# Attention of the first block: each pair of heads in three steps, of one group of two query tiles and two single ones, in place of four steps

## What is computed

```python
for l in range(DEPTH):                       # DEPTH = 2
    proj = rms_norm(x, attn_norm[l]) @ w_in[l]
    ...
    o_fox  = fox_attention(fq, fk, fv, cum_logf)          # 6 heads of 64, a forget gate added to the logits
    o_diff = diff_attention(dq, dk, dv, lam)              # 4 heads, two softmaxes of 32 dims each, p1 - lam * p2
    o_dsa  = dsa_attention(sq, sk, sv, iq, ik, iw, topk)  # 6 heads of 64, only the 128 best keys of a query
    x = x + concatenate([o_fox, o_diff, o_dsa]) @ w_out[l]
    gate, up = split(rms_norm(x, ffn_norm[l]) @ w_gate_up[l], 2)
    x = x + (silu(gate) * up) @ w_down[l]

# each attention, for a tile of 128 queries, causal:
p = softmax(where(mask, q @ k.T * scale (+ gates), -inf)); out = p @ v
```

## Time and profile before

| | |
|---|---|
| median of three runs | 2233.86 us |
| the profiled execution | 2233.64 us |
| its span | 2231.7 us |
| PE busy | 2178.9 us, 98% of the span |
| PEld, DVE, ACT, POOL busy | 1786.5, 1263.0, 901.3, 291.8 us |
| first layer's attention, from its first turn to its last values | 155.6 to 282.6 us |
| second layer's attention | 823.8 to 950.8 us |

### The profile page before, as it was taken

How to read it: one execution, slowest core, us unless ns; L and a number is a source line. 1 busy time by engine, 2 the same in 40 slices (tenths; PEclk the granted TensorE clock), 3 DMA queues, 4 the chain that set the end, 5 groups by cost and what they waited for, 6 DMA issues and landing times.

```text
span 2231.7 us, 31549 instructions
## 1 busy us (share of the span) xinstructions
PE 2178.9 (98%) x12794; PEld 1786.5 (80%) x12794; DVE 1263.0 (57%) x1751; ACT 901.3 (40%) x1574; POOL 291.8 (13%) x215
## 2 busy tenths in 40 slices
PE   7999999999999999999999999999999999999998
PEld 6886688778888776688778888989888887888777
DVE  5687648983224687648984226422666636212794
ACT  3447843222213447843222223232565524212673
POOL 3001213121222001322121000000010000000230
PEclk9999999999999999999999999999999999999999
DMA  5220016543563220016543321132000122321221
GB/s 164 90 71 2 1 57 207 173 148 86 143 176 93 90 71 1 2 59 205 182 145 81 138 96 58 49 98 75 16 23 9 53 76 92 123 70 57 72 72 57
DMA packets 149107, 194.28 MB, mean 87 GB/s; under 512 B 43165, under 2 KB 96426, under 8 KB 148962
## 3 DMA queue, kind: packets, MB, share of 16 engines
q1 hardware_dynamic: 110288, 169.83, 23.3%
q10 hardware_dynamic: 38514, 22.26, 3.7%
q0 software_dynamic: 160, 0.16, 0.0%
HBM read 180.51 MB, written 11.72 MB: 86 GB/s over the span
## 4 chain that ended last, share of the span: by engine, by line
PE 90%; DVE 4%; ACT 3%; issue 2%; DMA 0%; ACTq 0%; POOLq 0%; DVEq 0%
PE ps L535 69%; PE ps L2757 3%; PE ps L1890 3%; PE ps L2774 2%; PE ps L2786 2%; PE ps L2304 1%; PE ps L2261 1%; PE ps L2290 1%; DVE probs_t L2105 1%; PE ps L2762 1%; PE ps L1924 1%; ACT probs_t L2863 1%; DVE neg_max L2072 1%; PE ps L542 1%; PE ps L2760 1%
## 5 line engine op out<-in xcount | busy, mean ns | idle before, releaser
L500 DVE TENSOR_TENSOR w_low<-w_raw,w_high 128x2048 fp32r<-128x2048 f32 (+4 forms) x140 | 303.4, 2167 | 487.5 <-ACT w_high L495 487.3
L495 ACT ACTIVATE w_high<-w_raw 128x2048 fp32r<-128x2048 f32 (+4 forms) x140 | 253.2, 1809 | 577.2 <-PE ps L535 560.6
L535 PE MATMUL ps<-h_hi,w_high 128*128 128x512 f32 (+1 forms) x1168 | 439.7, 376 | 3.1 <-DVE w_low L500 2.1
L535 PE MATMUL ps<-h_lo,w_high 128*128 128x512 f32 (+1 forms) x1168 | 437.2, 374 | 0.0
L535 PE MATMUL ps<-h_hi,w_low 128*128 128x512 f32 (+1 forms) x1168 | 436.7, 374 | 0.0
L535 PEld LDWEIGHTS ps<-h_hi,w_high 128*128 128x128 f32 x1168 | 219.9, 188 | 53.9 <-issue 10.7
L535 PEld LDWEIGHTS ps<-h_hi,w_low 128*128 128x128 f32 x1168 | 219.8, 188 | 39.6
L535 PEld LDWEIGHTS ps<-h_lo,w_high 128*128 128x128 f32 x1168 | 220.0, 188 | 39.1 <-issue 0.5
L535 PE MATMUL ps<-w_high,h_hi 128*128 128x512 f32 (+3 forms) x576 | 214.2, 372 | 0.6 <-DVE h_lo L3159 0.6
L535 PE MATMUL ps<-w_low,h_hi 128*128 128x512 f32 (+3 forms) x576 | 211.6, 367 | 0.0
L535 PE MATMUL ps<-w_high,h_lo 128*128 128x512 f32 (+3 forms) x576 | 211.4, 367 | 0.0
(11 more groups left out here) (389 smaller groups left out, 3681.6 us busy)
## 6 DMA issues: line engine op xcount, KB each, us to landing
w_raw<-in_w_gate_up SPq DMA_DIRECT2D x44, 1024.0 KB, 5.2
ada_w<-in_ada_w SPq DMA_DIRECT2D x24, 1024.0 KB, 5.2
w_raw<-in_w_down SPq DMA_DIRECT2D x20, 1024.0 KB, 4.8
w_raw<-in_w_in SPq DMA_DIRECT2D x16, 1024.0 KB, 5.1
w_raw<-in_c_in_w SPq DMA_DIRECT2D x16, 1024.0 KB, 5.7
w_raw<-in_w_out SPq DMA_DIRECT2D x8, 1024.0 KB, 4.8
w_raw<-in_ab_in_w SPq DMA_DIRECT2D x8, 1024.0 KB, 5.1
masked_scratch<-mask_table ACTq DMA_DIRECT2D x8, 512.0 KB, 3.5
```

Source lines behind the costliest of these rows:

```text
L495: e.activation(w_high[j % 2][:, 0:size], w_raw[j % 2][:, 0:size], ACT.Copy).then_inc(sig.w_high_done, 1)
L500: e.tensor_tensor(w_low[j % 2][:, 0:size], w_raw[j % 2][:, 0:size], w_high[j % 2][:, 0:size].bitcast(F32), ALU.subtract).then_inc(sig.w_lo ...
L535: mm = e.matmul(dst, lhs, rhs, start=start and a == 0, stop=stop and a == 2)
```

## The change

A unit now has three steps instead of four. Step 3u holds the query tiles 1 and 0 side by side in one bank for each head (256 + 128 = 384 columns), step 3u + 1 holds tile 2 (384) and step 3u + 2 tile 3 (512). Maxima and exponentials stay one for each tile; transposes, their copy and the values of a step go together. There are three buffers for the transposed probabilities instead of two. For tile 0 the mask and the gates are written ahead of the scores and the scores are added; the copy of the causal mask that the kept keys of tile 0 use moves to keep_mask[:, 1, 256:384]. exps signals each head by itself. The loops run over units, each in two halves: on TensorE scores and masks of step 3u, transposes of the previous unit's steps 1 and 2, a first event of bank 7, values of the previous unit's step 0, a second event, scores and masks of steps 3u + 1 and 3u + 2, transposes of step 3u, the previous unit's wide, and its values of steps 1 and 2. VectorE's 37 rounds are spread over 15 halves, two or three behind the maxima of a half. The square root moves in ScalarE's order to the last unit's first half, and both pair_wide, both pair_finish and the last invert stand behind that unit.

```diff
-        probs1 = [at(f"probs1_{i}", [P, 2, S], F32, PJ_END + 4096 * i) for i in range(3)]
-        probs_t1 = [at(f"probs_t1_{i}", [P, 2, S], F32, PJ_END + 12288 + 4096 * i) for i in range(2)]
+        probs1 = [at(f"probs1_{i}", [P, 2, n], F32, PJ_END + 3072 * i) for i, n in enumerate((384, 384, 512))]
+        probs_t1 = [at(f"probs_t1_{i}", [P, 2, n], F32, PJ_END + 10240 + 3072 * i) for i, n in enumerate((384, 384, 512))]
...
-AHEAD, SETS = 2, 3
-ROUND_STEPS = 30
-EARLY_PARTS = {32: 0, 33: 1, 36: 2}
+TILES = ((1, 0), (2,), (3,))
+PER = len(TILES)
+ROUND_HALVES = 15
+EARLY_PARTS = {16: 0, 17: 1, 18: 2}
...
+        self.group(p, [("q", col(FQ + P * p)), ("k", col(FK + P * p))])
+        self.group(3 + 2 * c, [("q", col(DQ + P * c)), ("k", col(DK + P * c))])
+        self.group(7 + p, ([("d", lambda t: keys_twice[:, t, :])] if p == 0 else []) + [("q", col(SQ_ + P * p))])
+    self.steps = [(u, tiles) for u in range(len(self.units)) for tiles in self.TILES]
...
+    self.first_half = {u: [] for u in range(-1, U + 1)}
+    for i, (u, *_) in enumerate(self.turns):
+        self.first_half[u].append(("turn", i))
+    self.first_half[U - 1] += [("sum", 0), ("sum", 1)]
+    self.first_half[U] += [("pair_wide", 0), ("pair_wide", 1)]
+    for u in range(-1, U + 1):
+        for event in self.first_half[u] + ([("wide", u - 1)] if u > 0 else []):
...
+        self.turns.append((first - 1, dst, src, g))
...
+def parts(self, s):
+    at_ = 0
+    for t in self.steps[s][1]:
+        yield t, at_, (t + 1) * P
+        at_ += (t + 1) * P
...
 def bank(self, s, m):
+    return 2 * (s % self.PER) + m
...
 def tensor(self, e, B, L, ch):
+    def added(s, m, t, a, w, start, stop):
+        u, tiles = self.steps[s]
+        out_ = ps[:, self.bank(s, m), a:a + w]
+        if self.units[u].kind == "dsa":
+            at_ = a if t == 0 else 0
+            return e.matmul(out_, ident_r[:], keep_mask[:, tiles[0], at_:at_ + w], start=start, stop=stop)
+        return e.matmul(out_[:, w - P:w], ident_r[:], causal_r, start=start, stop=stop)
+    def gated(s, m, t, a, w, stop):
+        h = 2 * self.units[self.steps[s][0]].n + m
+        return e.matmul(ps[:, self.bank(s, m), a:a + w], gate_sel[:, h * P:(h + 1) * P], gate_t[:, 0:w], start=False, stop=stop)
 def scores(s):
+        u, tiles = self.steps[s]
+        x, parts = self.units[u], list(self.parts(s))
+        if s >= self.PER:
+            e.wait_ge(sig.turned_second, B["turned_second"] + s - self.PER + 1)
...
+        first = len(parts) == 2
+        if first:
+            for m in range(2):
+                added(s, m, *parts[1], True, False)
+                if x.kind == "fox":
+                    gated(s, m, *parts[1], False)
+        for t, a, w in reversed(parts):
+            last = first and t == 0
+            for m in range(2):
+                e.matmul(ps[:, self.bank(s, m), a:a + w], q[x.rows(m), t * P:t * P + P], k[x.rows(m), 0:w], start=not last, stop=bool(last))
+    def masks(s):
+        u, tiles = self.steps[s]
+        x, part = self.units[u], next(self.parts(s))
+        if x.kind == "dsa" and x.n == 0:
+            e.wait_ge(sig.keep_ready, B["keep_ready"] + tiles[0])
     for m in range(2):
+            mm = added(s, m, *part, False, x.kind != "fox")
     if x.kind == "fox":
         for m in range(2):
+                mm = gated(s, m, *part, True)
 def turn_probs(s):
     for m in range(2):
+            e.wait_ge(sig.probs_ready, B["probs_ready"] + 2 * s + m + 1)
+            for b in range(self.size(s) // P):
+                mm = e.transpose(ps[:, self.bank(s, m), b * P:(b + 1) * P],
+                                 probs1[s % 3][:, m, b * P:(b + 1) * P], ident)
 def values(s):
...
+        for t, a, w in self.parts(s):
+            for kt in range(t + 1):
+                for m in range(2):
+                    mm = e.matmul(ps[64 * m:64 * m + 64, 6, t * P:(t + 1) * P], x.value(m, kt),
+                                  probs_t1[s % 3][:, m, a + kt * P:a + (kt + 1) * P], start=kt == 0, stop=kt == t)
...
+    for u in range(-1, self.U + 1):
+        inside, events = 0 <= u < self.U, self.first_half[u]
+        if inside:
+            scores(3 * u)
+            masks(3 * u)
+        if u == 0:
+            keep_warm(e, 6, 6)
+        if u > 0:
+            turn_probs(3 * u - 2)
+            turn_probs(3 * u - 1)
+        for kind, i in events[0:1]:
+            event(kind, i)
+        if u < 0:
             keep_warm(e, 6, 5)
+        if u > 0:
+            values(3 * u - 3)
+        for kind, i in events[1:]:
+            event(kind, i)
+        if u < 0:
+            keep_warm(e, 6, 5)
+        if inside:
+            scores(3 * u + 1)
+            scores(3 * u + 2)
+            masks(3 * u + 1)
+            masks(3 * u + 2)
+        if u == 0:
+            keep_warm(e, 6, 4)
+        if inside:
+            turn_probs(3 * u)
+        if u > 0:
+            wide(u - 1)
+            values(3 * u - 2)
+            values(3 * u - 1)
...
 def scalar(self, e, B, L, ch):
 def exps(s):
...
+        if s >= self.PER:
+            e.wait_ge(sig.probs_turned, B["probs_turned"] + s - self.PER + 1)
     for m in range(2):
+            for t, a, w in self.parts(s):
+                c = 2 * NT * u + 2 * t + m
+                ins = e.activation(probs1[s % 3][:, m, a:a + w], ps[:, self.bank(s, m), a:a + w], ACT.Exp,
+                                   bias=neg_max[:, c:c + 1], accum_out=sums[:, c:c + 1])
+                if t != tiles[-1]:
+                    ch.step(ins)
+            ins.then_inc(sig.probs_ready, 1)
 def copy_probs(s):
...
+        if s >= self.PER:
+            e.wait_ge(sig.o_ready, B["o_ready"] + s - self.PER + 1)
+        e.activation(probs_t1[s % 3][:], self.both(s, 0, self.size(s)), ACT.Copy).then_inc(sig.turned_second, 1)
...
+    for u in range(-1, self.U + 1):
+        inside, turned = 0 <= u < self.U, [i for kind, i in self.first_half[u] if kind == "turn"]
+        if u > 1:
+            copy_o(u - 2)
+        if u > 0:
+            copy_probs(3 * u - 2)
+            copy_probs(3 * u - 1)
+        for i in turned[0:1]:
+            copy_turned(i)
+        if inside:
+            exps(3 * u)
+        for i in turned[1:]:
+            copy_turned(i)
+        if u == self.U - 1:
+            root()
+        if 2 * u in self.EARLY_PARTS:
+            high_part(self.EARLY_PARTS[2 * u])
+        if inside:
+            exps(3 * u + 1)
+            copy_probs(3 * u)
+        if u > 0:
+            copy_wide(u - 1)
+        if inside:
+            exps(3 * u + 2)
+        if u > 1 and self.units[u - 2].kind == "diff":
+            shift(u - 2)
+        if 2 * u + 1 in self.EARLY_PARTS:
+            high_part(self.EARLY_PARTS[2 * u + 1])
+    copy_o(self.U - 1)
...
 def vector(self, e, B, L, ch):
 def maxima(s):
...
+        for t, a, w in self.parts(s):
+            c = 2 * NT * u + 2 * t
+            ins = e.tensor_reduce(out=neg_max[:, c:c + 2], in_=self.both(s, a, w), op=ALU.max, axis=AX.X, negate=True)
+            if t != tiles[-1]:
+                ch.step(ins)
+        ins.then_inc(sig.max_ready, 1)
...
+    for h in range(2 * self.U + 1):
+        u = h // 2
+        if h == 2 * self.U:
+            for c in range(2):
+                pair_finish(c)
+            invert(u - 1)
+            break
+        if h % 2 == 0:
+            maxima(3 * u)
+            if u:
+                invert(u - 1)
+        else:
+            maxima(3 * u + 1)
+            maxima(3 * u + 2)
+        share = min(rounds, early + (rounds - early) * (h + 1) // self.ROUND_HALVES)
     while done < share:
         top_round(e, ch, 1 + done // ROUNDS)
...
```

More of the change, by code:

```diff
@@ L1107, in vector @@
                         e.wait_ge(sig.parts_ready, B["parts_ready"] + 4)
-                        ch.step(e.tensor_copy(keep_mask[:, 0, 0:P], cst("causal")[:, 384:512]))
+                        ch.step(e.tensor_copy(keep_mask[:, 1, 2 * P:3 * P], cst("causal")[:, 384:512]))
                     if i == self.groups - 1:
@@ L2758, in scores @@
-                    for m in range(2):
-                        if x.kind == "dsa":
-                            mm = e.matmul(ps[:, self.bank(s, m), 0:n], ident_r[:], keep_mask[:, t, 0:n], start=False, stop=True)
-                        else:
-                            mm = e.matmul(ps[:, self.bank(s, m), t * P:n], ident_r[:], causal_r, start=False, stop=x.kind != "fox")
+                    first = len(parts) == 2
[4 more added lines that the diff above has]
+                                gated(s, m, *parts[1], False)
@@ L2811, in pair_wide, with event @@
                     mm.then_inc(sig.pair_wide, 1)
-                for s in range(-4, self.N + 1):
-                    if 0 <= s + self.AHEAD < self.N:
-                        scores(s + self.AHEAD)
-                    if -2 <= s < 1:
-                        keep_warm(e, 6, 2 * s + 6 if s < 0 else 4)
-                    if 0 <= s < self.N:
-                        turn_probs(s)
```

(35 more changed lines are left out.)

94 lines of the change are left out of this document (15 added, 79 removed).

## The result

The changed kernel takes 2238.45 us (median of 20 runs, 2233.25 to 2240.74), the kernel before 2233.82 (20 runs beside it): a ratio of 1.0017, 95% interval 1.001 to 1.0023. That is slower, and at the edge of the 0.2% named ahead: the ratio lies inside it, while the medians are 4.63 us apart, and 2238.45 is just above the 2238.3 of the prediction's band. It is also above the forecast's own range of 2228 to 2237. An execution that ran far longer at a much lower mean clock, one of 2887 us among those of e1, is left out of the ratios. The profiled execution took 2238.79 us, 5.15 more than that of before; its span is 2237.0.

A forecast was written before the change was run, and what follows sets the result against it. TensorE, busy 98% of the span, was taken as the bound, with VectorE and ScalarE close behind. Unit terms summed to -0.8 us a layer, -1.6 for both, from 2233.64 to 2232 us; own range 2228 to 2237 (0.46), outer range 2221 to 2242.

The forecast's parts named there:

- the prediction's band: Whole kernel: times from 2229.4 to 2238.3 us, within 0.2% or 4.5 us, count as no change.
- at full clock: Attention stages: rows read at full clock while the widest tile's rounds run; no term for a lower clock.
- The periods: Unit lengths in one layer: units 0 to 2 -0.6 us, 3 to 6 -1.1, 7 and 8 -1.6, the end +2.5.
- under 12.0: Fox units 1 and 2: 12.4 us each; forecast wrong if their periods are under 12.0 or over 13.0.
- the mark on copies: Forecast wrong if TensorE waits for the copy of step 3u in units without rounds of tile 3.
- the second turn: Units 0, 1, 2, 4 and 6: second turned operand waits 0.6 us for ScalarE's copy, bounds 0 to 1.0.
- TensorE's prices: Cost per group on TensorE: fewer groups and moved wide save 0.6 us a unit; diff unit 9.5 us without turns.
- the forecast's +2.5: Unit 9 and the end: table loads ahead of last exponentials, then an uncovered chain; 20.1 us, +2.5 a layer.
- A: Rival, attention stages: handovers fit, TensorE's content alone decides; 2218 us, half of it 2225; chance 0.32 together with C.
- B: Rival, units 1 to 6: rounds ahead of step 3u + 1's maxima decide; +4.8 us a layer, 2242; chance 0.22.
- C: Rival, the end: table loads don't hold step 29's exponentials, 2 x 2.5 us goes; 2227; chance 0.32 with A.
- "same" and "faster": Whole kernel's chances: same (2229.4 to 2238.3 us) 0.46, faster 0.32, slower 0.22.

The follow-up runs named there:

- e1: Changed kernel with products that change no result filling six of TensorE's waits in each attention stage; 2230.84 us, 0.9985 of the kernel before.
- e2: Changed kernel with the last 28 values ahead of the last wide, as in the old order; 2231.34 us, 0.9983 of the kernel before.
- e5: Changed kernel with e2's end and VectorE's rounds moved forward, no block of three rounds of the widest tile; 2217.80 us, 0.9925 of the kernel before.
- e9: e5 with the second turn moved behind the masks of step 3u + 2 in units 0, 1, 2, 4, 6; 2213.77 us, 0.9905 of the kernel before.
- e7: Kernel before the change, with VectorE's rounds five at a time behind every fourth step instead of one or two behind each; 2323.43 us, single execution.
- e8: Kernel before the change, with its VectorE rounds moved forward in the same measure as in e5; 2237.70 us, 1.0014 of the kernel before.
- e6: e5 with six filling products behind unit 0's first transposes, in its long wait; 2217.76 us, 0.9926 of the kernel before.

## Why the prediction was wrong, step by step

**The clock, which was the step that failed.** The sum has TensorE "at full clock" and takes each wait at its own length. The waits themselves it foresaw: for the copy of step 3u in units 3, 5 and 6, for the keep in unit 7, for the spread at the end. That the products behind such a wait would run at 1.2 GHz stood in no term and in no rival, and it is what turned a gain into a loss: of the 5.2 us by which the profiled span grew, -4.7 are the periods, +8.4 the clock, and 1.6 lie outside the stages. With the clock held up (e1) the kernel takes 2230.84 us, inside the forecast's range. The runs of after bear it out, too: of the 20 executions of after, one with a mean granted clock of 0.996 took 2233.25 us, those with 0.992 and 0.993 took 2238.6 to 2240.7.

The Trainium skill, "TensorE: Matmul & The Clock Gate", section "A second HAM failure mode: psum-queue depth-cycling", says of one kernel that its TensorE, idle briefly but often between groups of products, swung between the two clock levels. The traces here don't bear out that it is the number of waits: two a unit of 0.3 to 0.4 us kept 1.00 before, and after, with fewer but longer ones, the means are 0.94 and 0.96.

**The periods.** At full clock (e1, second layer, from the scores of tile 1 of one unit to those of the next) against the prediction: unit 0 10.55 for 11.0; fox units 1 and 2 11.82 and 11.61 for 12.4 each; unit 3 9.92 for 10.1; unit 4 11.19 for 11.1; 5 and 6 11.57 and 11.72 for 11.5 and 11.6; unit 7 12.72 for 12.7; unit 8 9.92 for 10.4; the end 20.05 for 20.1, counted as the forecast did from unit 9's first scores (19.72 from those of tile 1). The mechanism of most held: VectorE had no idle time in unit 5, the block of three stood between TensorE and its copy, the keep came late in unit 7. The fox units were mis-sized by up to 0.8: by the mark set ahead ("under 12.0") that term is wrong. Met too is the mark on copies: ahead of unit 1's scores TensorE waits 1.06 us for the copy of step 0, and unit 0 has no rounds of tile 3, though the prediction's own chain for unit 0 had that wait in it. Of the 0.8, 0.2 is the second turn, whose wait was not 0.6:

```profile
847.00 0.66 PE L2754 MATMUL ps<-con,proj 128*128 128x128 f32 x4 [0.36 <-ACT q_turned L2892]
```

The rest is content, most of it the scores (next paragraph). All errors over 0.1 lie on one side, and at full clock the stages came out 2.1 and 2.6 us shorter than before where 0.8 was forecast. One term was missing the other way: with masks and gates ahead of tile 0's scores, a stage's first scores come 3.25 us behind its first product, against 2.78 before. (The terms for unit 3 add up to 10.2, not 10.1.)

**TensorE's prices.** 14 transposes to the next group 1.65 (887.96 to 889.61; 1.64 forecast), 12 values 0.80, 6 transposes and the wide 1.21 (892.61 to 893.82), both as forecast. The group costs that the prediction read from the earlier trace rows for transposes and values carry over to larger groups. What it overlooked is that scores have one too. Its own prices of 0.41, 0.62, 0.84 and 1.06 us rise by 0.22 a tile, which leaves 0.19 for the group, and scores also fall from four groups to two. The scores of tiles 2 and 3 together take 1.70 (890.41 to 892.11), where 1.90 was forecast, those of tiles 0 and 1 0.85 (886.83 to 887.68) for 1.03, and four masks in a row 0.50 (892.11 to 892.61) for 0.56. So a diff unit has 9.0 us of TensorE's work instead of 9.5: this term was mis-sized by nearly 0.5 us in every unit. (The eight changes of tiling mode that the prediction counts for the new unit are those of a unit with a second turn between values and scores; without it there are seven.)

**VectorE.** The timeline of unit 5, second layer: 

```profile
888.66 1.01 DVE L2979 TENSOR_REDUCE neg_max<-ps 128x2 f32<-128x512 f32 x2
...
890.00 0.68 DVE L2642 MAX8 top<-score 128x8 f32<-128x512 f32 x1
...
891.73 0.70 DVE L2642 MAX8 top<-score 128x8 f32<-128x512 f32 x1
...
893.47 0.69 DVE L2642 MAX8 top<-score 128x8 f32<-128x512 f32 x1
...
894.98 2.08 DVE L2979 TENSOR_REDUCE neg_max<-ps 128x2 f32<-128x768 f32 x2
```

Rounds of 1.73, 1.74 and 1.51 us, as read ahead. ScalarE, in the same place and then at the root:

```profile
895.97 0.58 ACT L2902 ACTIVATE probs<-ps,neg_max 128x384 f32<-128x384 f32 x1 [3.62 <-DVE neg_max L2979]
897.09 0.81 ACT L2912 ACTIVATE probs_t<-ps 128x768 f32<-128x768 f32 x1
...
940.73 1.28 ACT L2941 ACT_TABLE_LOAD   x1
...
942.83 1.28 ACT L2902 ACT_TABLE_LOAD   x1
```

It waits 3.62 us for the maxima behind the three rounds, and the copy that follows at 897.09 is what TensorE waits for until 898.04. At the end the two table loads do stand ahead of the last exponentials. The end grew from 17.63 us to 20.05 at full clock, close to the forecast's +2.5. But the loads aren't what made it long: e2, with the loads where they were, takes 18.19, so 1.9 of the 2.4 us came from the order of wide and values.

**The rivals.** A needed the handovers to fit; they don't in units 0 and 3 to 7. That e5 reaches its 2218 (2217.8) is in part luck: e5 still waits 0.7 to 1.3 us ahead of three units of the first layer and four of the second, and it has the cheaper end of e2. B, that the rounds' block decides in every unit, fails in units 1 and 2, behind which TensorE doesn't wait for a copy; its price of 4.8 us a layer didn't come, and that the time came out towards its side is due to the clock. C was refuted by the end of 20.05 us, though e2 shows that its gain was there to be had from another order. The chances of "same" and "faster" were too high for a reason that no case carried: a change that merges two short waits into one long was priced as neutral.

What stays open: what makes a drop follow one wait (2.47 us at 898.04) and not another (2.54 at 920.73), and what brought the drop at 270.6. e9 had one drop of 3.4 us in its first stage and none in its second, though the longest waits were alike (2.19 and 2.15 us). Length tells for the odds alone. In the profiles of the nine kernels of the new order other than e1 (two have unit 0's wait filled) there are 18 waits of 2 us and more in the stages, and 14 have a drop that begins within them or up to 2.5 us behind; of 23 waits between 1 and 2 us, 6 have. One drop of 21 in these stages, that at 270.6, has no such wait ahead of it.

## What to carry to other kernels

On a TensorE that is busy for over 90% of a stage, count the length of each single wait, not only their sum: two waits of 0.3 us a unit kept full clock, while behind a wait of 2 us and more there mostly were several us of half clock (14 of 18), at a third of a us for each. Larger groups save their group cost (0.13 us each for transposes and values here, 0.19 for scores), but what an engine is handed in larger portions comes later, so the work between the portions (here the rounds on VectorE) has to be given out anew; together, and with the old order at the end, they brought 0.75% (0.9925), while the grouping alone and such rounds alone were both slower than before. Look at the granted clock of every stage before you believe a sum of durations.

## What the runs showed of the hardware that was not expected

The granted clock of TensorE had only the levels 0.5 and 1.0 in these stages, and its low stretches lasted between 3.4 and 20.5 us. In after it fell behind single waits of 1.06 to 2.84 us in stages in which TensorE was 90% busy, and it fell in the order of before too once its waits were made long (e7, waits of 1.03 to 10.3 us ahead of its drops); it didn't fall in either stage of before (no wait over 0.41 us) nor of e8 (one of 0.8). It isn't the same from one execution to the next: after spread over 7.5 us in 20 runs. Products that do nothing, put into the waits, kept it at 1.00 in e1 and made the kernel faster by 7.6 us; a single filled wait (e6) made no difference in the median.
